# First tap of a causal depthwise convolution: from VectorE to ScalarE, with the weight splits issued after the taps

## The reference

```python
def causal_dwconv(u, w, bias):
    s = u.shape[1]
    upad = jnp.pad(u, ((0, 0), (CONV_WIDTH - 1, 0), (0, 0)))
    out = bias
    for j in range(CONV_WIDTH):
        out = out + w[j] * upad[:, j:j + s]
    return out
...
        h = rmsnorm(x, norm_ffn_g[l])
        u = causal_dwconv(h @ w_up[l], conv_w[l], conv_b[l])
        gate, val = jnp.split(u, 2, axis=-1)
        x = x + (jax.nn.silu(gate) * val) @ w_down[l]
```

## Time and profile before

| | us |
|---|---|
| median of 3 runs | 2026.54 |
| lowest and highest | 2024.76, 2027.18 |
| the profiled execution | 2031.31 |
| its span in the trace | 2029.4 |
| TensorE busy in the span | 1861.8 (92%) |
| VectorE busy | 1167.6 (58%) |
| ScalarE busy | 648.5 (32%) |
| granted TensorE clock, mean | 0.959 |

### The profile page before, as it was taken

How to read it: one execution, slowest core, us unless ns; L and a number is a source line. 1 busy time by engine, 2 the same in 40 slices (tenths; PEclk the granted TensorE clock), 3 DMA queues, 4 the chain that set the end, 5 groups by cost and what they waited for, 6 DMA issues and landing times.

```text
span 2029.4 us, 23515 instructions
## 1 busy us (share of the span) xinstructions
PE 1861.8 (92%) x8254; PEld 1489.2 (73%) x8254; DVE 1167.6 (58%) x1772; ACT 648.5 (32%) x960; POOL 201.2 (10%) x150
## 2 busy tenths in 40 slices
PE   5887989999999999999899998877789999999996
PEld 4665777777888888888677776666567788888874
DVE  6447658888534755532443776576683755452266
ACT  4333412222223222222333334444353322222242
POOL 3121000000000000000033344243000000000000
PEclk9888999999999999999899999977899999999997
DMA  3431222223222222323222331310152222232221
GB/s 136 79 67 42 73 80 89 92 92 101 100 98 83 93 93 97 103 100 100 78 83 73 114 129 59 114 68 32 47 161 83 73 96 101 93 119 100 92 71 54
DMA packets 55340, 180.61 MB, mean 89 GB/s; under 512 B 6216, under 2 KB 6984, under 8 KB 55272
## 3 DMA queue, kind: packets, MB, share of 16 engines
q1 hardware_dynamic: 43200, 157.07, 23.2%
q10 hardware_dynamic: 12072, 22.67, 4.0%
HBM read 167.65 MB, written 12.06 MB: 89 GB/s over the span
## 4 chain that ended last, share of the span: by engine, by line
PE 68%; DVE 19%; issue 6%; ACT 3%; DMA 2%; POOL 1%; DVEq 1%; ACTq 0%; SPq 0%; POOLq 0%
PE bank L721 16%; PE bank L722 16%; PE bank L723 16%; PE bank L743 2%; PE bank L744 2%; PE bank L809 2%; PE bank L745 2%; PE bank L810 2%; PE bank L811 2%; DMA raw<-in_w_proj 1%; DVE sq L1990 1%; PE bank L1078 1%; PE bank L789 1%; DVE w_lo L1711 1%; DVE chunk L1809 1%
## 5 line engine op out<-in xcount | busy, mean ns | idle before, releaser
L1142 ACT ACTIVATE w_hi<-raw 128x1024 fp32r<-128x1024 f32 (+2 forms) x281 | 304.4, 1087 | 742.7 <-PE bank L723 677.8
L721 PE MATMUL bank<-a_hi,w_hi 128*128 128x512 f32 x1272 | 504.1, 396 | 17.9 <-DVE w_lo L1711 7.7
L723 PE MATMUL bank<-a_hi,w_lo 128*128 128x512 f32 x1272 | 496.8, 391 | 0.0
L722 PE MATMUL bank<-a_lo,w_hi 128*128 128x512 f32 x1272 | 496.5, 390 | 0.0
L1711 DVE TENSOR_TENSOR w_lo<-raw,w_hi 128x1024 fp32r<-128x1024 f32 (+2 forms) x219 | 280.4, 1281 | 246.7 <-ACT w_hi L1142 234.2
L721 PEld LDWEIGHTS bank<-a_hi,w_hi 128*128 128x128 f32 x1272 | 239.9, 189 | 87.9 <-issue 19.7
L723 PEld LDWEIGHTS bank<-a_hi,w_lo 128*128 128x128 f32 x1272 | 239.7, 188 | 50.7
L722 PEld LDWEIGHTS bank<-a_lo,w_hi 128*128 128x128 f32 x1272 | 240.1, 189 | 49.4 <-issue 1.0
L633 POOL TENSOR_TENSOR w_lo<-raw,w_hi 128x1024 fp32r<-128x1024 f32 x54 | 130.5, 2419 | 1103.9 <-ACT w_hi L1142 1103.9
L721 PE MATMUL bank<-h_hi,w_hi 128*128 128x512 f32 x568 | 221.1, 389 | 0.2 <-DVE w_lo L1711 0.2
L723 PE MATMUL bank<-h_hi,w_lo 128*128 128x512 f32 x568 | 221.0, 389 | 0.0
(11 more groups left out here) (291 smaller groups left out, 2255.3 us busy)
## 6 DMA issues: line engine op xcount, KB each, us to landing
raw<-in_w_up SPq DMA_DIRECT2D x132, 512.0 KB, 3.4
raw<-in_w_down SPq DMA_DIRECT2D x48, 704.0 KB, 4.0
raw<-in_w_proj SPq DMA_DIRECT2D x59, 512.0 KB, 3.5
raw<-in_w_wo SPq DMA_DIRECT2D x8, 512.0 KB, 3.4
raw<-in_w_branch SPq DMA_DIRECT2D x16, 256.0 KB, 2.7
gates_in<-spill ACTq DMA_DIRECT2D x16, 256.0 KB, 3.0
raw<-in_w_out SPq DMA_DIRECT2D x8, 512.0 KB, 4.3
raw<-in_w_ple SPq DMA_DIRECT2D x8, 512.0 KB, 3.5
```

What stands on the lines that cost most here:

```text
L721: mm(dst[:, :], wh, hi[:, k, :], start=(first and c == 0), stop=False)
L722: mm(dst[:, :], wh, lo[:, k, :], start=False, stop=False)
L723: step = mm(dst[:, :], wl, hi[:, k, :], start=False, stop=(last and c == n - 1))
L1142: fn(w_hi[:, slot, 0:size], raw[:, slot, 0:size], ACT.Copy).then_inc(unit_high, 1)
```

## The change

ScalarE makes the tap on the token itself, with the bias, as one activation `Identity` with a scale and a bias per partition, straight into `gate` or `val`. VectorE's `tensor_scalar` goes; it waits for the new semaphore `tap_ready` instead. VectorE's split of a unit moves from between the eviction and the taps to behind the taps (except the one of unit 5 in turn 0). On ScalarE the silu of a pair now comes between the pair's two new activations, and each `w_hi` stands behind a tap.

```diff
@@ scalar
             def silu_pairs(i, it=0, per_loop=0):
                 first = UNIT["up1"][0]
+
+                def tap(name, tile):
+                    at = PARAMS[name][0] + tile
+                    return par[:, bass.ds(it * 4 + at, 1)]
+
+                def last_tap(tile, dst):
+                    act.wait_ge(tile_sem("up1", tile), TILE["up1", tile][1] + 1 + it)
+                    fn(dst[:, :], sq[:, 0, :], ACT.Identity, bias=tap("conv_b", tile),
+                       scale=tap("conv_w2", tile)).then_inc(tap_ready, 1)
+
                 for j in (i, i + 1):
+                    last_tap(2 * j, gate)
                     if j != 1:
                         units_done(first + 2 * j + 1, it, 2 * per_loop)
+                    act.wait_ge(gate_ready, j + 1 + it * per_loop)
+                    fn(silu[:, :], gate[:, :], ACT.Silu).then_inc(silu_ready, 1)
+                    last_tap(2 * j + 1, val)
                     if j:
                         units_done(first + 2 * j + 2, it, 2 * per_loop)
-                    act.wait_ge(gate_ready, j + 1 + it * per_loop)
-                    fn(silu[:, :], gate[:, :], ACT.Silu).then_inc(silu_ready, 1)
@@ vector
                         dve.wait_ge(tile_sem("up1", tile), TILE["up1", tile][1] + 1 + it)
-                        if i >= skip:
-                            split_unit(first + 4 * turn + i + 3, it, 4)
                         if skip and i == 1:
                             split_unit(first + 5)
-                        step(v.tensor_scalar(dst[:, :], b[:, :], tap("conv_w2", i), tap("conv_b", i), ALU.mult,
-                                             ALU.add), it, per)
+                        dve.wait_ge(tap_ready, tile + 1 + it * 4)
                         step(v.scalar_tensor_tensor(dst[:, 1:T], b[:, 0:T - 1], tap("conv_w1", i), dst[:, 1:T],
                                                     ALU.mult, ALU.add), it, per)
                         step(v.scalar_tensor_tensor(dst[:, 2:T], b[:, 0:T - 2], tap("conv_w0", i), dst[:, 2:T],
                                                     ALU.mult, ALU.add), it, per)
                         if n == 0:
                             dve.sem_inc(gate_ready, 1)
+                        if i >= skip:
+                            split_unit(first + 4 * turn + i + 3, it, 4)
```

More of the change, by code:

```diff
@@ L540, in two_blocks @@
         high_done = sem("high_done")
+        tap_ready = sem("tap_ready")
         silu_ready = sem("silu_ready")
@@ L1975, in _ @@
             first = UNIT["up1"][0]
-            per = 14
+            per = 10
             b = sq[:, 0, :]
```

## The result

| | before | changed |
|---|---|---|
| median, us (runs) | 2025.67 (4) | 2043.54 (4) |
| lowest and highest | 2024.76, 2027.18 | 2042.69, 2044.36 |
| ratio to before, 95% interval | | 1.0089 [1.0074, 1.0104] |
| span of the profiled execution | 2029.4 | 2041.0 |

The change makes the kernel slower by 0.89% [0.74%, 1.04%], some 18 us; a second timing gave 0.81% [0.67%, 0.95%], 16.1 us between the medians. Forecast were 2039.0 us, +12.5 us, and a range of 2031.5 to 2045.5.

The account below looks back on a forecast made before the run. VectorE's queue was taken to bound up1's loop at 22.67 us a turn; 40 tiles at 0.25 us (+10.0) plus 2.5 us at the stage's end gave +12.5 us, from 2026.54 to 2039.0 us, range 2031.5 to 2045.5.

Parts of the forecast that it names:

- The bound: Loop of up1: VectorE's queue sets the turn at 22.67 us; TensorE, 0.98 us a turn faster, follows.
- The sum: Whole kernel: 40 tiles of up1 at 0.25 us, +10.0 us, plus 2.5 us at its end, +12.5 us.
- the round trip: Each tile in up1's loop: VectorE to ScalarE and back takes 1.07 us against 0.81 us, +0.26 us a tile.
- The second tile of turn 0: Start of up1, before the loop: counted like the other tiles, at +0.25 us.
- The second operand: ScalarE's new activation: scale plus bias make it 0.80 us, against 0.708 us with one per-partition operand.
- The split's new place: VectorE in up1's loop: the split only changes its place, its 1.14 us being paid behind the taps.
- The cover of w_hi: ScalarE in up1: w_hi takes 1.06 us of the 2.02 us from tap's end to split, 0.96 us to spare.
- The end of the stage: End of up1, unit 43: its split ends 4.45 us behind the eviction's start instead of 1.96, costing +2.5 us.
- The rival of the faster kernel: up1's loop: VectorE's turn falls to 19.9 us, TensorE bounds, 8.8 us less, 2017.7 us; chance 0.05.
- No change: Rival in up1: hand-off costs no more than the tensor_scalar's 0.81 us, only 2.5 us remain, 2029.0 us; chance 0.08.
- slower by more: Rival in up1: ScalarE not free when the tile comes, 0.3 us more a tile, 12 us, 2051; chance 0.07.
- tables: Rival on ScalarE: Identity and Silu need different tables, so every pair would reload them twice; chance 0.01.

Follow-up runs that it names:

- the run with cover: Changed kernel with VectorE's split back between eviction and taps and each w_hi in front of ScalarE's tap: 2016.24 us against 2026.93 before, ratio 0.9955.

## Why the prediction was right, point by point

- **The bound.** Right. VectorE's queue set the turn; both the run with cover and the changed kernel say so from either side.
- **The sum.** Direction and range right, size 12.5 us where `up1` lost 15.9 and the medians say 16 to 18. The term that was mis-sized is the round trip, "0.12 + 0.80 + 0.15 = 1.07 us": it measured 0.18 + 0.82 + 0.14 = 1.14. 0.06 of the 0.07 lie in the way to ScalarE: I took the 0.09 us of the earlier trace rows and added 0.03 for a register instruction as short as that of the earlier trace rows, and here the instruction was 0.08 us long with 0.07 behind it. 36 x 0.07 = 2.5 us, and 0.4 us more come from taking 0.25 for 0.26; together 2.9 of the 3.0 us that the loop lost beyond its 9.0. Outside the loop the hole was 0.95 us, not 0.86, because the second tap waits for two semaphores and one wait goes to the sequencer, as in the earlier trace rows, so that the way back took 0.10 us, not 0.03: 0.1 us more at the end of the stage, and in turn 0, with its second tile, 0.2.
- **The second tile of turn 0.** Right in size by luck. It was counted with the others at +0.25 us and lost 0.22, but its split never moved, so the round trip could have been covered there and the tile have gained. The run with cover shows it: there the second tap starts 1.18 us behind the eviction's end, not 1.97. The prediction looked for table loads in the loop alone; the one in front of the first silu costs the changed kernel about 1.97 - 1.18 = 0.8 us.
- **The second operand.** Right. Each costs 0.09 us on the mean: 0.63 us without, 0.82 with two. The rule of the Trainium skill, "ScalarE: Activation LUTs", "What ACT_TABLE_LOAD costs", gave an estimate of 0.80 us; the trace has 0.82 and decides, and the nearest row alone, 0.71, would have been wrong. The 0.15 us that a computed address costs in the loop come on top of the activation's record.
- **The split's new place.** "The split only changes its place" was right for the changed kernel, where the register work runs under the round trip, and wrong as a general statement: alone, the move costs 0.08 us a tile.
- **The cover of w_hi.** Right. It ends at 403.52 + 1.04 = 404.56, and the split starts at 405.53, 0.97 us later; 0.96 had been forecast. No split in the loop waits for it.
- **The end of the stage.** Right: 2.6 us where 2.5 were forecast.
- **The rival of the faster kernel.** It failed here for the reason given, that the order left VectorE nothing to do, and the run with cover is that rival with the order put right: it gained 9.1 us where 8.8 had been worked out, and VectorE's turn fell to 19.8 to 19.9 us as forecast. The Trainium skill's rule ("VectorE: DVE Perf Modes", "Rules for kernel authors": in chained VectorE instructions keep down their number, not that of the semaphores) does not settle it: both kernels have one VectorE instruction less a tile, and one is 16 to 18 us slower and the other 9 us faster, depending on what fills the time until the other engine is done.
- **No change; slower by more; tables.** None came. There is no table load in the loop, and the one in turn 0 is in both kernels.

## What to carry to other kernels

Moving an instruction off the engine that bounds a stage pays only if that engine has something to do until the result comes back. Here 0.81 us of a `tensor_scalar` with its gaps became a 1.14 us hole, and the kernel 16 to 18 us slower; with the split, 1.14 us that were at hand all the time, kept in the hole and its `w_hi` made in time, the same move gained 9 us. When two edits come together, look which of them takes away what the other needs, and on the helping engine check what stands in front of the wanted result.

## What was not expected of the hardware

- The register instruction that works out the two operands' addresses costs 0.15 us on ScalarE between the wait and the start (1.14 against 0.99 us of idle time); its own record is 0.08 long. On VectorE that of the first tap costs 0.08 us a tile behind the eviction (0.20 against 0.12 us), and nothing where it runs under the split.
- In a stage 800 us behind the change, with the same instructions, the granted clock was 0.79 in all three profiles with the first tap on VectorE and 0.84 to 0.87 in the six with it on ScalarE. The stage is 3.3 us shorter in the changed kernel's profile, a fifth of the effect that was to be measured. The cause is open, and so is whether the executions without a profile share it; a difference of two profiled spans is therefore no measure of a change this small.
